# Each expert's result added to the output by two indirect DMAs of 512 columns, in place of one of 1024

## What is computed

```python
def swiglu(t, w_up, w_down):
    gate, up = split_cols(t @ w_up, (w_down.shape[0], w_down.shape[0]))
    return (jax.nn.silu(gate) * up) @ w_down
...
    def step(acc, blk):
        ...
        y = swiglu(u_pad[tok], w_exp_up[e], w_exp_down[e])
        return acc.at[tok].add(y.astype(jnp.float32) * w_of_slot[slots][:, None]), None
...
    shared = swiglu(u, w_shared_up, w_shared_down).astype(jnp.float32)
    return (routed + shared).astype(u.dtype)
```

## Time and profile before

| | us |
|---|---|
| median of 3 runs | 1241.75 (1240.92 to 1246.57) |
| the profiled execution's own time | 1239.8 |
| span of its trace | 1238.0 |
| PE busy, share of the span | 92% |
| DVE | 72% |
| ACT | 58% |
| POOL | 21% |

### The profile page before, as it was taken

One profiled execution on the slowest core, in us unless ns is written; L12 is line 12 of the kernel. 1 busy time (PEld: TensorE's weight loads), 2 busy tenths in 40 slices (PEclk: granted clock), 3 DMA queues, 4 the chain that ended last, 5 costly groups with the idle time before them and its releaser, 6 DMA issues.

```text
span 1238.0 us, 15884 instructions
## 1 busy us (share of the span) xinstructions
PE 1140.3 (92%) x5707; PEld 866.0 (70%) x5707; DVE 892.9 (72%) x1133; ACT 723.8 (58%) x926; POOL 258.3 (21%) x145
## 2 busy tenths in 40 slices
PE   4999998989999899998999999999999999999993
PEld 3699987767677687775777676666666666666772
DVE  4576378545443585687999888888888888888991
ACT  7543333334333422413888787777877878777881
POOL 1000000000000000001233343433434343334451
PEclk9999998999999999999999999999999999999997
DMA  6313222221212323368999999999999999999942
GB/s 216 129 52 102 86 94 69 68 69 34 68 34 68 140 94 102 125 271 312 377 362 359 370 369 370 369 371 368 370 368 373 366 376 368 371 357 343 363 95 38
DMA packets 74519, 285.90 MB, mean 231 GB/s; under 512 B 10868, under 2 KB 33416, under 8 KB 49620
## 3 DMA queue, kind: packets, MB, share of 16 engines
q1 hardware_dynamic: 59716, 251.16, 54.0%
q0 software_dynamic: 14736, 33.87, 11.6%
HBM read 272.39 MB, written 29.38 MB: 244 GB/s over the span
## 4 chain that ended last, share of the span: by engine, by line
DMA 47%; PE 38%; DVE 6%; issue 5%; ACT 2%; POOL 0%; SPq 0%; POOLq 0%; DVEq 0%; ACTq 0%
DMA out_dram<-arena 46%; PE bank L1466 29%; PE bank L1634 2%; PE bank L1661 2%; PE bank L1545 1%; PE bank L1646 1%; DMA arena<-in_x_dram 1%; ACT front_split L568 1%; ACT arena L568 1%; DVE front_split L903 1%; DVE arena L1001 0%; DMA arena<-u_rows,arena 0%; DVE hT_low L909 0%; DMA arena<-in_w_in_dram 0%; PE bank L1624 0%
## 5 line engine op out<-in xcount | busy, mean ns | idle before, releaser
L1373 DVE TENSOR_TENSOR low<-arena,high 128x2048 fp32r<-128x2048 f32 x192 | 438.9, 2287 | 72.2 <-ACT high L568 71.1
L568 ACT ACTIVATE high<-arena 128x2048 fp32r<-128x2048 f32 x192 | 367.2, 1913 | 0.7 <-PE bank L1466 0.5
L1466 PE MATMUL bank<-high,gatheredT 128*96 128x512 f32 x1024 | 325.4, 399 | 9.0 <-DVE gatheredT L1380 8.8
L529 POOL DMA_INDIRECT arena<-u_rows,arena x64 | 117.9, 1842 | 600.5 <-DVE arena L1368 561.7
L1466 PEld LDWEIGHTS bank<-high,gatheredT 128*96 128x96 f32 x1024 | 161.2, 162 | 77.4 <-issue 8.1
L537 POOL DMA_INDIRECT out_dram<-arena x64 | 134.4, 2099 | 364.4 <-DMA out_dram<-arena 341.3
L1466 PE MATMUL bank<-low,gatheredT 128*96 128x512 f32 x512 | 202.7, 396 | 0.0
L1466 PE MATMUL bank<-high,hidT 128*96 128x512 f32 x512 | 168.3, 411 | 1.9 <-DVE hidT L1398 1.9
L568 ACT ACTIVATE arena<-bank 96x512 f32<-96x512 f32 (+4 forms) x217 | 107.9, 531 | 104.5 <-DMA out_dram<-arena 35.4
L1466 PE MATMUL bank<-hT_high,front_split 128*128 128x512 f32 x448 | 143.9, 402 | 0.8 <-DVE hT_low L909 0.8
L1466 PEld LDWEIGHTS bank<-low,gatheredT 128*96 128x96 f32 x512 | 82.9, 162 | 36.3
(11 more groups left out here) (253 smaller groups left out, 1428.5 us busy)
## 6 DMA issues: line engine op xcount, KB each, us to landing
arena<-in_w_exp_up_dram SPq DMA_DIRECT2D x128, 1024.0 KB, 17.0
arena<-in_w_exp_down_dram SPq DMA_DIRECT2D x64, 1024.0 KB, 17.8
arena<-in_w_in_dram SPq DMA_DIRECT2D x14, 1024.0 KB, 5.3
arena<-in_w_in_dram SPq DMA_DIRECT2D x10, 768.0 KB, 4.5
arena<-in_w_branches_dram SPq DMA_DIRECT2D x4, 1024.0 KB, 5.1
arena<-in_w_out_dram SPq DMA_DIRECT2D x4, 1024.0 KB, 5.0
arena<-in_x_dram SPq DMA_DIRECT2D x4, 512.0 KB, 5.5
arena<-in_w_mem_kv_dram SPq DMA_DIRECT2D x2, 1024.0 KB, 5.3
```

Of the source, the lines that this page charges most:

```text
L529: pool.indirect_dma_start(gathered[0:ROWS, e % 2, :], None, u_dram, bass.IndirectOffsetOnAxis(ap=index[0:ROWS, e:e + 1], axis=0), bounds_c ...
L568: return nc.scalar.activation(o, i, ACT.Copy, **kw)
L1373: v.tensor_tensor(low_part[k % SLOTS], raw[k % SLOTS], high_part[k % HIGHS].bitcast(F32), ALU.subtract).then_inc(low_done, 1)
L1466: ins = mm(bank, left[a], right[b], start=first and q == 0, stop=last and q == 2)
```

## The change

`added` and `y_ready` become two semaphores each, one for each half of the 1024 columns. `scatter(e, h)` adds columns 512h to 512h+511 of the result. It sees the output as 1024 rows of 512 values, and takes its row numbers from `half_index`, which is 2 x token + h. It waits for `y_ready[h]` and for the last scatter of the same half only. ACT waits and counts by half as well: the copy of half h waits for `added[h]` of expert `e-2` and gives `y_ready[h]`. PE waits for `y_ready[1]`. DVE makes `half_index` with two more operations before it gives `index_ready`.

```diff
-            def scatter(e, r):
-                wait_pass(y_ready, r, E, e + 1)
+            def scatter(e, h, r):
+                wait_pass(y_ready[h], r, E, e + 1)
                 if not isinstance(r, int) or e >= 1:
-                    wait_pass(added, r, 16 * E, 16 * e)
-                pool.indirect_dma_start(out_rows, bass.IndirectOffsetOnAxis(ap=index[0:ROWS, e:e + 1], axis=0),
-                                        y_out[0:ROWS, e % 2, :], None, bounds_check=bound, oob_is_err=False,
-                                        compute_op=ALU.add).then_inc(added, 16)
+                    wait_pass(added[h], r, 16 * E, 16 * e)
+                pool.indirect_dma_start(out_halves, bass.IndirectOffsetOnAxis(ap=half_index[0:ROWS, h, e:e + 1], axis=0),
+                                        y_out[0:ROWS, e % 2, 512 * h:512 * (h + 1)], None, bounds_check=half_bound,
+                                        oob_is_err=False, compute_op=ALU.add).then_inc(added[h], 16)
...
-                    scatter(e, r)
-                wait_pass(added, r, 16 * E, 16 * E)
+                    for h in range(2):
+                        scatter(e, h, r)
+                for h in range(2):
+                    wait_pass(added[h], r, 16 * E, 16 * E)
...
-                if not isinstance(m, int) or m >= 2:
-                    act.wait_ge(added, m * 16 - 16)
-                copy(y_out[0:ROWS, n % 2, 0:512], ps[4][0:ROWS, :])
-                copy(y_out[0:ROWS, n % 2, 512:1024], ps[6][0:ROWS, :]).then_inc(y_ready, 1)
+                for h in range(2):
+                    if not isinstance(m, int) or m >= 2:
+                        act.wait_ge(added[h], m * 16 - 16)
+                    copy(y_out[0:ROWS, n % 2, 512 * h:512 * (h + 1)], ps[4 + 2 * h][0:ROWS, :]).then_inc(y_ready[h], 1)
...
-                v.tensor_scalar(index[0:ROWS, :], ps[7][0:ROWS, 0:E], NO_TOKEN, None, ALU.add).then_inc(index_ready, 1)
+                v.tensor_scalar(index[0:ROWS, :], ps[7][0:ROWS, 0:E], NO_TOKEN, None, ALU.add)
+                for h in range(2):
+                    last = v.tensor_scalar(half_index[0:ROWS, h, :], ps[7][0:ROWS, 0:E], 2.0, 2 * NO_TOKEN + h, ALU.mult, ALU.add)
+                last.then_inc(index_ready, 1)
...
-                    pe.wait_ge(y_ready, m)
+                    pe.wait_ge(y_ready[1], m)
```

More of the change, by code:

```diff
@@ L129, in build @@
         index = at(take(E), E).bitcast(U32)
+        half_index = at(take(2, E), 2, E).bitcast(U32)
         slot_w = at(take(E), E)
@@ L292, in build @@
             sem, ("tanh_done", "act_ready", "hid_ready", "hidT_done", "hidT_high", "hidT_low"))
-        y_ready, added = map(sem, ("y_ready", "added"))
+        y_ready = [sem(f"y_ready{h}") for h in range(2)]
+        added = [sem(f"added{h}") for h in range(2)]
         groups = [("qf", QB, 512), ("qa", QA, AW), ("ka", KA, AW), ("va", VA, AW), ("ib", IB, BV), ("og", OG, BV),
@@ L505, in _ @@
             pool.dma_start(out_norm, bcast(io["out_norm_b"], P, BV)).then_inc(c_in[7], 16)
-            bound = pool.to_reg(T - 1)
-            out_rows = out.rearrange("a t d -> (a t) d")
+            bound, half_bound = pool.to_reg(T - 1), pool.to_reg(2 * T - 1)
+            out_halves = out.rearrange("a t (h d) -> (a t h) d", h=2)
             turn = pool.alloc_register("passes_done")
@@ L1365, in read_deal @@
                 if not isinstance(r, int):
-                    dve.wait_ge(added, r * (16 * E))
+                    for h in range(2):
+                        dve.wait_ge(added[h], r * (16 * E))
                 v.tensor_reduce(slot_w[0:ROWS, :], ps[7][0:ROWS, E:3 * E].rearrange("p (v e) -> p e v", v=2), AX.X, ALU.add)
-                v.tensor_scalar(index[0:ROWS, :], ps[7][0:ROWS, 0:E], NO_TOKEN, None, ALU.add).then_inc(index_ready, 1)
+                v.tensor_scalar(index[0:ROWS, :], ps[7][0:ROWS, 0:E], NO_TOKEN, None, ALU.add)
+                for h in range(2):
+                    last = v.tensor_scalar(half_index[0:ROWS, h, :], ps[7][0:ROWS, 0:E], 2.0, 2 * NO_TOKEN + h, ALU.mult, ALU.add)
+                last.then_inc(index_ready, 1)
             def low(k, u):
@@ L1825, in deal_sets @@
                 else:
-                    pe.wait_ge(y_ready, r * E)
+                    pe.wait_ge(y_ready[1], r * E)
                 for g in range(SETS):
```

## The result

The changed kernel takes **1229.21 us** (median of 4 runs, 1226.49 to 1230.33), the kernel before 1241.58 us (4 runs, 1240.92 to 1246.57). The ratio is 0.9889, with a 95% interval of 0.9858 to 0.9919: faster, by 12.4 us, where the forecast was 1222 us and the range 1207 to 1257. The profiled execution took 1229.39 us.

What follows compares the result with a forecast made beforehand. The chain of scatters was taken as the bound, weights close behind. Limits of 28 us (chain) and 27 us (weights), less 8 us and the half microsecond, left 20 us: 1219.8 profiled, 1222 us as median, range 1207 to 1257.

Steps and rivals of the forecast that it cites:

- The transfer term: Scatter cycle: a half scatter moves half the bytes and so lands sooner, taken as 0.7 us off the cycle.
- The queue term: Scatter cycle: the software queue holds three DMAs instead of two, taken as 0.2 us more per cycle.
- POOL's offsets: Issue times within a cycle: second half's chain 2.4 us behind the first, gather issued at about 4.8 us.
- rival (b): Software queue: it gets full, so the gather delays the next first half; for example +25 us, 1266 us; chance 14%.
- g: Software queue: time needed between a gather's landing and the next first half's; from 4.0 us the cycle is longer than now.
- The DMA engines: Weight loading: extra packets cost 5 us, last weights land about 2 us later, gain at most 27 us.
- The 8 us taken off: Sum: a deduction, guessed at a third, because two limits of nearly the same size are not both reached.
- the forecast's cause: Main case: cycle 9.3 to 9.95 us or the weights as limit, time 1207 to 1235 us, given 65%.
- The chances at the end: Outcome against the kernel before, with about 0.5% as no change: faster 0.64, same 0.21, slower 0.15.
- The small things: Start and end of the path: index operations +0.3 us, earlier first scatter -0.5, last half +0.7, sum +0.5.
- (a): Scatter landing: it does not depend on size, so the cycle stays 10.17 us and the time 1241; chance 18%.
- (c): DMA engines: an accumulating row costs by the row, so 4096 more rows give 1308 us; chance 3%.

Runs made afterwards that it cites:

- e1: The changed kernel without the second half's scatters, so columns 512 to 1023 are left out and nothing waits for them: 1195.86 us in one run.
- e5: The kernel before with odd experts' scatters added to a second DRAM buffer, merged at the end, so consecutive scatters are independent: 1243.02 us, ratio 0.9990.
- e9: The changed kernel with the second scatter moving 16 columns per row in place of 512, still 96 rows: 1192.27 us in one run.
- e11: The changed kernel with DVE making each low part in four quarter operations in place of one: 1228.23 us, ratio 0.9875 to the kernel before.
- e8: The changed kernel with the first half waiting until both halves of the expert before have landed: 1290.27 us in one run.
- e7: The changed kernel gathering only rows 0 to 47 of each expert, both scatter halves kept whole: 1226.85 us in one run.
- e4: The kernel before with each weight block loaded by two DMAs of 4 KB per partition instead of one of 8 KB: 1234.00 us, ratio 0.9918.
- e6: The changed kernel with every weight block loaded by two DMAs of 4 KB per partition instead of one of 8 KB: 1230.93 us in one run.

## Why the prediction was right, and where not

**What bounds the kernel** was read rightly. The chain of scatters was the bound, as e1 shows by taking from it (47 us of 1242.67 gone, PE never idle in the middle), and the weights lay close behind, as e5 shows (chain gone, weights the limit).

**The transfer term**, -0.7 us, was too large: -0.51 us behind the issue in e1. That the whole landing falls by 0.73 us there is luck, since 0.22 of it are POOL's issue, for which the sum has no term. The row's price was too high as well. An accumulating row of 4096 bytes takes 327 ns and one of 2048 bytes 176 ns, where 90 us per MB give 369 and 184; a gathered row takes 195 ns, where I let it cost what weights cost, 168. With 64 rows on 16 engines the two measured prices give 0.60 us for the half.

**The queue term** is the step that failed. I put +0.2 us on the third DMA in the queue and it costs 0.6: 9.18 us in the changed kernel against 8.58 in e1, 0.11 of it on POOL and 0.49 behind the issue. That leaves 0.13 us per landing and 0.19 per cycle, so 11 us over 57 cycles in place of 28. I had taken a whole cycle's slack of 7 us before a scatter as room, without adding up what the new DMA brings into it. The second half takes a gap of some 3.3 us, and the next first half follows 3.3 us behind the gather. The trace of e9 puts most of the 0.49 us on the third DMA as such: without its bytes, 0.36 of them are still there. A sum that stood open to me, three DMAs at the 3.3 us which lie between a scatter's and a gather's landing in the trace of before, gives an estimated 9.8 us, over the 9.67 us that I put down for the cycle. It would have been a warning and no more, since single gaps of the changed kernel are as short as 2.4 us.

**POOL's offsets** were too small. The second half goes 3.37 us behind the first (I said 2.4), the gather 5.82 us (4.8); POOL's busy time rose by 143 us (about 130). The gather lands after 10.02 us, at 15.8 us of the cycle instead of 14.9. This is rival (b)'s place: by its formula 15.84 + 3.31 - 9.18 = 9.97 us, which must come out so once all three are measured. With these landings the kernel would be slower than before from g = 10.17 - 15.84 + 9.18 = 3.5 us (with those I had assumed, from 4.0). It was 3.3, and so the sign stayed, by little. That the queue **needs** this g, which is (b)'s mechanism, is not shown.

**The DMA engines.** The packets came as worked out: 7168 more in the software queue. In 640:1120 the queues show this, beside the earlier trace rows:

```profile
q1 hardware_dynamic: 20587, 149.93, 80.6%
q0 software_dynamic: 16238, 24.77, 22.5%
```

The weights still cost 41 us of engine time per MB. The software queue costs 22.5% x 7680 / 24.77 = 70 us per MB, where it was 66. On its 33.89 MB that is 4.2 x 33.89 / 16 = 9 us for the stage, and I took 5 of "8 at most". The last weights came 6.1 us later, not 2. The gain of this limit was not 27 us but, with the 7.3 us that e5 and e11 show can't be gained, about 28.7 - 7.3 - 6.1 = 15 us. e11, which runs into it, ends there.

**The 8 us taken off** because two near limits are not both reached stand for nothing that was measured, since the changed kernel never waits for weights. They offset part of the terms that were too good. They also went off the 28 us of the chain and not off the smaller 27. Without them the forecast would have been 1214 us; with them it missed by 7 us. So the time in the range is in part luck, and some 3 us of the 10.5 between the two traces are the closing drain.

**The signs.** The time lies in the 1207 to 1235 us of the forecast's cause, but its cycle does not lie in the 9.3 to 9.95 us that belong to it, if only by 0.03 to 0.04. Of what I had named as signs, POOL's busy time and ACT's shorter waits came. A cycle of 9.6 to 9.7 us, a landing of 8.6 to 8.8, a last block split within 10 us (it was 15.1) and waits of ACT for weights did not. The chances at the end do not follow from the text either: 0.65 less a tenth of it is 0.585 for faster, and not 0.64.

**The small things** were of the right size: the first scatter 0.9 us earlier where I had 0.2. The 4 us lost in the tail were missing from the sum, though the last part of the stretch, where weights still load, was in view.

**The rivals.** (a) would have been read out of the trace of the changed kernel alone, 9.18 us against 9.31, with the cycle a little shorter; only e1 refutes it. (c) is refuted by 176 ns for a row of 2048 bytes against 327 for 4096. The Trainium skill (*DMA: Bandwidth & Descriptors*, "Anatomy of one DMA") gave an estimated 0.3 us for what a half saves. The runs show 0.73 us by itself, 0.51 of it behind the issue, and 0.13 us where the other half stands in the same queue. "They serialize", which the Trainium skill says there under "Rules for kernel authors" of halves of the partitions, and here the halves are columns, agrees with landings that follow each other at some 3.3 us, and yet the change gains, since each half waits for its own predecessor alone (with one wait for both it loses, e8).

**What stays open:** by what way the third DMA delays the first packet of the next half from 3.2 to 3.7 us; whether it is the bytes of the second half that shift POOL's issue against DVE's work, which is most of what e9 gains; how much POOL's issue in order holds (e7); and why the closing drain takes 3.4 us in some kernels and 6.5 in others.

## What to carry to other kernels

A chain of dependent DMAs is as long as its landings, and half of a landing may be waiting beside other traffic (4.7 of 9.4 us here): cutting each link into two halves with waits of their own saves only transfer (0.5 of 9.3 us here) and puts a further DMA into the same queue, which took back as much. Before such a split, take a landing apart into the issue, the wait before the first packet and the rest, and ask which of them the split touches. Then add up the landing gaps of all that the queue carries per cycle and compare the sum with the new cycle, as a warning. Price the next limit by the time from landing to use, less what passes there even when it binds, and less what the split adds to the engines' work.

## What the runs showed of the hardware

- An accumulating row takes 327 ns of a DMA engine at 4096 bytes, 176 at 2048 and 31 at 64, a gathered row of 4096 bytes about 195 (traces of before, the changed kernel, e9). A row beyond the bound still has a packet of 9 ns (median).
- From the end of POOL's indirect DMA instruction to the first packet 3.2 us pass beside a full stream of weight loads and 0.6 us without one, with the software queue empty before it (the kernel before). With a third DMA per cycle in the queue it is 3.7 us (the changed kernel, e9).
- Under a full stream of weight loads the size of that stream's packets sets how soon a scatter lands: 9.31 us behind packets of 8 KB, 8.66 behind packets of 4 KB (e4), with the whole gain behind the first packet, for about 2% of the stream's rate (10.14 us per expert for 9.94 in e5).
- Three DMAs of 96 rows per cycle in one software queue landed 3.0 to 3.5 us apart on average beside weight packets of 8 KB (the changed kernel, e11), single ones 2.0 to 5.5. With 64 bytes per row the gap was 2.7 us (e9), with half the rows of the gather 2.3 (e7), and beside packets of 4 KB 2.9, 2.3 and 4.7 (e6).
- POOL issues an indirect DMA in 1.4 us or in 2 to 3.5 us. DVE beside it is one cause (2.2 us with a `low` operation beside a scatter's issue and 1.44 without, in the kernel before), but shorter DVE operations brought nothing in one kernel (2.06 to 2.04 us) and 0.1 to 0.4 us in the other.
